# The input projection's token columns in three groups of 264, 512 and 512, and the weights' slots at the tokens' remainder modulo 512 bytes

## The reference

```python
for l in range(DEPTH):                       # DEPTH = 2
    h = _rmsnorm(x, norm1_g[l])
    z = h @ w_in[l]                          # (1024 x 1024) @ (1024 x 2824)
    mq, mk, mv, mi, mf, mo, aq, ak, av = split(z)
    qk = silu(causal_dwconv(concat(mq, mk)))
    hm = mlstm_chunkwise(...)                # 4 heads of 128, chunks of 64
    hm = _rmsnorm(hm) * sigmoid(mo)
    ha = swa_sinks(rope(rmsnorm(aq)), rope(rmsnorm(ak)), av)
    x = x + concat(hm, ha) @ w_out[l]
    h2 = _rmsnorm(x, norm2_g[l])
    x = x + square(relu(h2 @ w_ff1[l])) @ w_ff2[l]
```

## Time and profile before

| | |
|---|---|
| median of 3 runs | 2230.84 us (2230.73 to 2233.3) |
| profiled execution, its own time | 2231.89 us |
| its span | 2230.0 us |
| TensorE clock granted | 0.99 of the full clock |
| PE busy | 2140.7 us, 96% of the span |
| PEld, DVE, POOL, ACT busy | 1805.8, 1424.1, 988.0, 857.6 us |

### The profile page before, as it was taken

How to read it: one execution, slowest core, us unless ns; L and a number is a source line. 1 busy time by engine, 2 the same in 40 slices (tenths; PEclk the granted TensorE clock), 3 DMA queues, 4 the chain that set the end, 5 groups by cost and what they waited for, 6 DMA issues and landing times.

```text
span 2230.0 us, 34286 instructions
## 1 busy us (share of the span) xinstructions
PE 2140.7 (96%) x11748; PEld 1805.8 (81%) x11748; DVE 1424.1 (64%) x1674; ACT 857.6 (38%) x1459; POOL 988.0 (44%) x697
## 2 busy tenths in 40 slices
PE   6999998989999999999999999899899999999998
PEld 6998877878788877888899887788878887778886
DVE  4127865467777777676640488654677777876764
ACT  4224333345666642121231343432556666321210
POOL 3334524324555555445522455143245555454542
PEclk9999999999999999999999999899999999999999
DMA  7322225415777788776532223254166677987663
GB/s 261 105 92 76 72 94 179 136 70 168 255 254 241 239 304 314 306 281 256 215 129 86 90 77 111 83 174 151 39 209 237 237 237 249 348 313 292 270 273 142
DMA packets 227662, 427.29 MB, mean 192 GB/s; under 512 B 24936, under 2 KB 167016, under 8 KB 219248
## 3 DMA queue, kind: packets, MB, share of 16 engines
q1 hardware_dynamic: 212336, 402.93, 51.0%
q10 hardware_dynamic: 15232, 23.16, 2.9%
HBM read 272.79 MB, written 157.43 MB: 193 GB/s over the span
## 4 chain that ended last, share of the span: by engine, by line
PE 58%; issue 19%; POOL 12%; DVE 5%; ACT 2%; SPq 1%; DMA 1%; ACTq 1%; POOLq 0%; DVEq 0%
PE ps L1368 23%; PE ps L1714 20%; POOL w1s L1309 8%; PE ps L1553 7%; POOL w2s L1313 3%; PE ps L1666 1%; DMA uk<-uD 1%; PE ps L1472 1%; DVE y L1756 1%; DVE hT L1762 1%; PE ps L1499 1%; PE ps L1486 1%; PE ps L1591 1%; PE ps L1592 1%; PE ps L1359 1%
## 5 line engine op out<-in xcount | busy, mean ns | idle before, releaser
L1714 PE MATMUL ps<-w2s,uk 128*128 128x512 f32 x2688 | 618.6, 392 | 7.6 <-DVE uf L2249 4.1
L1714 PEld LDWEIGHTS ps<-w2s,uk 128*128 128x128 f32 x2688 | 504.8, 189 | 120.2 <-issue 11.4
L2213 DVE TENSOR_TENSOR xs<-ps,xs 128x1024 f32<-128x1024 f32 x208 | 253.4, 1222 | 171.6 <-PE ps L1714 169.9
L1666 PE MATMUL ps<-hT,w1s 128*128 128x512 f32 x1344 | 317.8, 392 | 10.6 <-DVE uf L2175 4.7
L1666 PEld LDWEIGHTS ps<-hT,w1s 128*128 128x128 f32 x1344 | 250.1, 188 | 73.4 <-issue 12.5
L1313 POOL TENSOR_TENSOR w2s<-raw,w2s 128x1024 fp32r<-128x1024 f32 x64 | 182.0, 2866 | 181.3 <-ACT w2s L1088 181.3
L1309 POOL TENSOR_TENSOR w1s<-rawf,w1s 128x512 fp32r<-128x512 f32 x112 | 170.2, 1531 | 194.3 <-ACT w1s L982 194.3
L1368 PE MATMUL ps<-hT,whi 128*128 128x512 f32 x768 | 246.3, 402 | 0.0
L1368 PE MATMUL ps<-whi,hT 128*128 128x258 f32 x1280 | 238.2, 286 | 1.0 <-DVE hT L1762 0.6
L1666 PE MATMUL ps<-tT,w1s 128*128 128x512 f32 x1008 | 237.3, 389 | 0.0
L1666 PEld LDWEIGHTS ps<-tT,w1s 128*128 128x128 f32 x1008 | 189.1, 188 | 39.5
(11 more groups left out here) (209 smaller groups left out, 3318.7 us busy)
## 6 DMA issues: line engine op xcount, KB each, us to landing
uk<-uD SPq DMA_DIRECT2D x64, 1024.0 KB, 8.7
raw<-in_wstream SPq DMA_DIRECT2D x104, 512.0 KB, 5.6
uk<-uD SPq DMA_DIRECT2D x64, 768.0 KB, 7.8
rawf<-in_wstream SPq DMA_DIRECT2D x64, 512.0 KB, 4.3
uD<-uh SPq DMA_DIRECT2D x64, 512.0 KB, 5.1
uD<-uf SPq DMA_DIRECT2D x64, 512.0 KB, 5.3
uD<-uh SPq DMA_DIRECT2D x64, 384.0 KB, 4.1
uD<-uf SPq DMA_DIRECT2D x64, 384.0 KB, 5.0
```

The costliest lines, as they stand in the source:

```text
L1666: mm = pe.matmul(ps[:, bank, :], w, x[:, k, :], start=(first and k == 0 and i == 0), stop=(k == 3 and i == 2), skip_group_check=True)
L1714: mm = pe.matmul(ps[:, bank + tp, :], u, w2s[r][:, w, k, :], start=(r in (1, 2, 5) and k == 0 and i == 0), stop=(k == 1 and i == 2), skip_ ...
L2213: V.tensor_tensor(y, ps[:, bank:bank + 2, :], y, ALU.add).then_inc(y_acc, 1)
```

## The change

The 1288 columns of stage A are in three groups, GC = 264, 512 and 512: 3 x 8 x 24 = 576 matmuls a layer. Group 0 takes the first 258 columns of z's store and its last six (from column ZX = 1282 on). The host's layout of the weights stays in pieces of 258 columns, so each unit is put together by two or three DMAs. Group 0 still has two units (of four k), groups 1 and 2 have four each (of two k). The high and low parts have places of their own: `ahi0`, `alo0` and `ahi1` where the slots were, `alo1` behind the small tables, `ahi2`, `alo2` in the place of x (`xs`), for which ACT waits until x is normed and stored. The slots of the later stages are 4096 bytes long, and all of them, `ahi1`, `alo1`, `ahi2`, `alo2`, `mxh` and `mxl`, now lie at 224 modulo 512. `ahi0` is at 224 and `alo0` at 480, with slices 1056 bytes apart. Other small tiles move by 128 bytes (`qS`, `kown`, `kw0`, `Cst` and so on). `zst` holds 512 columns.

```diff
+GC = (264, 512, 512)
+ZX = ZV + 512 - 6
...
-        raw = [ring_r(f"raw{s}", [P, 4 * GW], F32) for s in range(RING)]
+        raw = [ring_r(f"raw{s}", [P, 4 * GC[0]], F32) for s in range(RING)]
         hilo_at = ring_r.at
-        whi = [ring_r(f"whi{s}", [P, 4 * GW], F32R) for s in range(RING)]
-        wlo = [ring_r(f"wlo{s}", [P, 4 * GW], F32R) for s in range(RING)]
+        ahi0, alo0 = [ring_r(f"a{n}0", [P, KT, GC[0]], F32R) for n in ("hi", "lo")]
+        ahi1_at = ring_r.at
+        ahi1 = ring_r("ahi1", [P, KT, 512], F32R)
+        br = Region(hilo_at)
+        whi = [br(f"whi{s}", [P, D], F32R) for s in range(RING)]
+        br = Region(ahi1_at)
+        wlo = [br(f"wlo{s}", [P, D], F32R) for s in range(RING)]
+        xr_ = Region(wide.at)
+        ahi2, alo2 = [xr_(f"a{n}2", [P, KT, 512], F32R) for n in ("hi", "lo")]
...
+        alo1 = Region(ahi1_at + (ta.at - ahi1_at + 511) // 512 * 512)("alo1", [P, KT, 512], F32R)
...
-                sp.dma_start(raw[slot][:], wtoken[l, n]).then_inc(s_raw[slot], 16)
+                def piece(g, kh, k0, ks, c0, dst):
+                    src = wtoken[l, 2 * g + kh].rearrange("p (k c) -> p k c", c=GW)
+                    sp.dma_start(dst, src[:, k0:k0 + ks, c0:c0 + dst.shape[2]]).then_inc(s_raw[slot], 16)
+                if n < 2:
+                    d = raw[slot][:].rearrange("p (k c) -> p k c", c=GC[0])
+                    piece(0, n, 0, 4, 0, d[:, :, 0:GW])
+                    piece(4, n, 0, 4, ZX - 4 * GW, d[:, :, GW:GC[0]])
...
-                    nc.scalar.copy(zst[b][:], ps[:, G + t % 2, 0:GW]).then_inc(a_ev, 1)
+                    nc.scalar.copy(zst[b][:, 0:GC[g]], ps[:, G + t % 2, 0:GC[g]]).then_inc(a_ev, 1)
...
-                    if t in (2, 3):
-                        split_a(l, t, 0, 0)
+                    if 2 <= t < 6:
+                        if t == 2 and l > 0:
+                            act.wait_ge(y_m, l * YM)
+                        split_a(l, t)
...
-                group(1, 2)
-                rows_b()
-                group(2, 0)
+                for n in range(NT):
+                    tile(1, n)
+                    if n == 3:
+                        rows_b()
                 rows_t()
-                group(3, 2)
-                rows_m()
-                group(4, 0)
+                for n in range(NT):
+                    tile(2, n)
+                    if n == 3:
+                        rows_m()
```

More of the change, by code:

```diff
@@ L104, in trunk_kernel @@
         ta = Region(tmp_at)
-        zst = [ta(f"zst{b}", [P, GW], F32) for b in range(4)]
+        zst = [ta(f"zst{b}", [P, 512], F32) for b in range(4)]
         gN = ta("gN", [P, NT, 8], F32)
@@ L172, in trunk_kernel @@
         ends = Region((nc.sbuf_usable_end - 3 * 4 * D) // 32 * 32)
[L173 removed]
+        assert max(ta.at + 512 + 4 * KT * 512, tc.at) <= ends.at, (ta.at, tc.at, ends.at)
         ybuf = [ends(f"y{b}", [P, D], F32) for b in range(2)]
@@ L370, in unit_a @@
                 sp.wait_ge(w_lo, l * U + max(n + 1, RING))
-                sp.dma_start(raw[slot][:], wtoken[l, n]).then_inc(s_raw[slot], 16)
+                def piece(g, kh, k0, ks, c0, dst):
[5 more added lines that the diff above has]
+                    piece(4, n, 0, 4, ZX - 4 * GW, d[:, :, GW:GC[0]])
+                else:
+                    kh, k0 = (n - 2) % 4 // 2, (n - 2) % 2 * 2
+                    d = raw[slot][:, 0:D].rearrange("p (k c) -> p k c", c=512)
+                    if n < 6:
+                        piece(1, kh, k0, 2, 0, d[:, :, 0:GW])
+                        piece(2, kh, k0, 2, 0, d[:, :, GW:512])
+                    else:
+                        piece(2, kh, k0, 2, 512 - GW, d[:, :, 0:4])
+                        piece(3, kh, k0, 2, 0, d[:, :, 4:4 + GW])
+                        piece(4, kh, k0, 2, 0, d[:, :, 4 + GW:512])
             def unit(l, n, slot):
@@ L710, in landed, with unit_raw, unit_part, unit_hi @@
             eng.wait_ge(s_raw[slot], (l * (16 * per_layer[slot]) + use * 16) + 16 * (before + 1))
+        def unit_raw(n):
+            return raw[n % RING][:, 0:(4 * GC[0] if n < 2 else D)]
+        def unit_part(n, a0, a1, a2):
+            t, k = (a0, 4) if n < 2 else (a1 if n < 6 else a2, 2)
+            i = n if n < 2 else (n - 2) % 4
+            return t[:, i * k:(i + 1) * k, :].rearrange("p k c -> p (k c)")
+        def unit_hi(n):
+            return unit_part(n, ahi0, ahi1, ahi2)
+        def unit_lo(n):
+            return unit_part(n, alo0, alo1, alo2)
         @block.scalar
         def _(act):
-            def split_a(l, slot, before, use):
-                landed(act, l, slot, before, use)
-                nc.scalar.copy(whi[slot][:], raw[slot][:]).then_inc(w_hi, 1)
+            def split_a(l, n):
+                landed(act, l, n % RING, 2 * (n // RING) + (1 if n < 6 else 2), 0)
+                nc.scalar.copy(unit_hi(n), unit_raw(n)).then_inc(w_hi, 1)
             def split_hi(l, slot, before, use, dst):
@@ L1373, in _, with tile @@
             for l in range(DEPTH):
-                def tile(g, s0, n):
-                    pe.wait_ge(a_ev, l * (5 * NT) + g * NT + (n + 1))
+                def tile(g, n):
+                    pe.wait_ge(a_ev, l * (3 * NT) + g * NT + (n + 1))
                     t = tile_of(l * 2, n) if g == 0 else n
-                    pairs = []
+                    wh, wl = ((ahi0, alo0), (ahi1, alo1), (ahi2, alo2))[g]
                     for k in range(KT):
[L1381 to L1389, removed]
+                        if n == 0:
+                            if g == 0 and k == 0:
+                                pe.wait_ge(w_lo, l * U + (2 + RING))
+                            elif g > 0 and k % 2 == 0:
+                                pe.wait_ge(w_lo, l * U + (4 * g - 2 + k // 2 + 1 + RING))
+                        c = (t % 4) * P
+                        h_, l_ = hT[:, t // 4, 0, k, c:c + P], hT[:, t // 4, 1, k, c:c + P]
+                        for i, (a, b) in enumerate(((h_, wh), (h_, wl), (l_, wh))):
+                            mm = pe.matmul(ps[:, G + n % 2, 0:GC[g]], a, b[:, k, :], start=(k == 0 and i == 0), stop=(k == KT - 1 and i == 2))
+                    mm.then_inc(a_done, 1)
                 if l == 0:
```

73 lines of the change are left out of this document (40 added, 33 removed).

## The result

The changed kernel takes **2238.62 us** (median of 7 runs, 2236.36 to 2239.88) where the kernel before, run beside it, takes 2230.84 (7 runs, 2228.76 to 2234.17). The ratio is 1.0032 with an interval of [1.0022, 1.0042]: 7 us slower. 2224.2 was forecast. The profiled execution took 2238.57 us with a span of 2236.8, against 2231.89 and 2230.0.

What follows compares the result with a forecast made beforehand. PE, busy 96% of the span, was taken as the bound: matmul count by start distance. Gains 20.9 less losses 14.3 net 6.6 us off 2231.9; the median, 1.05 lower, gives 2224.2 us, range 2209 to 2235.

Steps and rivals of the forecast that it cites:

- Head, 14.0: Start of layer 0: small load pieces wait turns behind large packets, PE starts at 36.0 not 21.91; 14.0 us lost.
- Rival 1: Head: not late, as q1's packets are batched or 24-byte runs merged; 2210.8 us, chance 0.13.
- Stage A, 10.6: Stage A: fewer, wider matmuls at 226.7 ns save 5.3 us a layer, 10.6 us in all.
- ACT late in group 0, 0.25 a layer: Stage A, group 0: ACT's 4.2 us at tiles 2 to 4 exceed PE's 3.8; 0.5 us lost in all.
- Rival 3: Stage A: uncosted stalls, ACT late in group 0 or units 6 to 9 late; 4 us more, 2228, chance 0.16.
- POOL's low parts "have eight tiles of time": Stage A, groups 1 and 2: POOL's four low parts a group, 2.9 us each, are hidden; no loss.
- Stage B, 6.0: Stage B: 1152 matmuls each 6.2 ns shorter through operand placement, 7.1 us, of which 6.0 arrive.
- Stage C, 4.3: Stage C: 768 matmuls each 6.2 ns shorter through operand placement, 4.8 us, of which 4.3 arrive.
- Rival 2: B, C and wide groups: place in SBUF doesn't set the distance, which stays 232.9 ns; 2239 us, chance 0.13.
- The MLP, 0: MLP, to the next stage A or the end: no change in time, 0 us.

Runs made afterwards that it cites:

- the best version: Changed kernel with each stage A unit one load, group 0's evacuation one store, and splits of units 4 and 5 at tiles 6 and 7; 2216.01 us.
- e3: Changed kernel with the load of `gB` issued ahead of unit 0's two loads; ratio 1.0017 to the kernel before.
- e1: Changed kernel with each stage A unit laid out by the host as one run per partition, so one load; 2225.61 us.

## Why the prediction was wrong

It had the sign wrong, by 13.4 us of span: 2.1 of them in the head, 6.4 in stage A, 2.9 in B, 0.2 in C and 1.8 in the MLP. By its own steps:

- **Head, 14.0 (with bounds to 16).** The mechanism is right and shown twice (whole units, late copies). Unit 1's split began at 31.69 (about 32 forecast), and with `gB` first PE started at 36.27 (36.0). What was missing is 1.8 us: the prediction named `gB` and DVE's `y` as late "and catch up before unit 1's low part". They didn't, since each `y` stood still beside one of POOL's low parts (6.63 us for two of 1.27).
- **Rival 1** (packets batched) is out: 160 packets against 160.
- **Stage A, 10.6.** This size was right, where nothing else was in the way: the best version saves 5.4 and 5.5 a layer, for 5.3 in the sum. The distance of 226.7 ns was right too.
- **ACT late in group 0, 0.25 a layer.** This is the step that failed. The changed kernel's stage A lacks 127.91 - 126.16 = 1.75 in layer 0 and 131.55 - 126.35 = 5.2 in layer 1 to the best version's: 6.95 us for a term of 0.5, and all of it in group 0. The sum compared ACT's work in a tile (4.2 us, with 0.34 a store) with PE's 3.8, and let PE's lead over the evacuations cover it. The second issue took 0.45 to 1.35 us, and it stands between an evacuation and `norm_hi`, on the way by which PE gets its next tile; PE's lead doesn't help there. In layer 1 later low parts are worth 4.5 us with two stores and nothing (0.1) with one; one store is worth 6.3 with early low parts, 1.9 with late ones. So they cost most together: the second store puts DVE's `y` of tile 7 into the time of POOL's low part, `y` stands for 2 us, PE's gap grows to 2.5, and its clock falls for 3.4 us. The clock's part is about 1.5 us: e3, with a gap of 2.46 but no such stretch behind it, has 34.33 us in group 0 where the changed kernel has 35.84. Rival 3 was this mechanism, priced at 4 us with a chance of 0.16.
- **POOL's low parts "have eight tiles of time".** True for POOL, but DVE waits for it. The prediction asked only if POOL was late. Beside a whole low part `y` took 3.28 us (in e1), beside halves 2.22 and alone 1.27, while `hT`'s low part took its 1.23 beside one (at 1151.40). The Trainium skill's page SBUF — State Buffer (section SBUF: two separate sides) has the rule: GpSimd and a VectorE operation with two inputs in SBUF use one pair of ports, and whoever starts first keeps it for the whole instruction. The trace agrees: `y` (from `xs` and `gB`) and `gN` (from `zst` and `rowp`) are such operations, the low part `hT` (one input from PSUM) is not.
- **Stage B, 6.0.** 3.1 came in the changed kernel. The distance is right (5.48 a unit, 0.11 less; 0.15 forecast): the first matmuls of the unit at 173.91, behind the attention's small ones, start 230, 231, 236, 228, 233 and 231 ns apart, and only then come 226 and 227. 48 units by 0.11 are 5.3, of which 3.1 arrived. In layer 0 one more half-clock stretch fell into the dense part of the stage, at 304 us; the other kernels with these slots took 188.0 to 189.9 there, and over both layers these kernels gained 2.8 to 4.8.
- **Stage C, 4.3**: 4.1, which is in part luck. The ten other kernels with these slots gained 1.5 to 4.0 there. Rival 2 is out for B, C and the wide groups.
- **The MLP, 0.** It is the same program and took 1.7 us longer in layer 1. The windows show where: before, and then after, 19 us behind the first matmul of the stage.

```profile
1598.00:1604.00 6.00, 5.41 (x46) 5.41 (x47) 3.27 (x5) 1.45 (x3) 1.28 (x1) 1.00 0.00 0
```

```profile
1603.00:1609.00 6.00, 5.57 (x34) 5.57 (x35) 2.80 (x4) 0.02 (x1) 1.28 (x1) 0.72 0.00 0
```

34 matmuls in place of 46, at a mean clock of 0.72: half clock for some 3.4 us. In the profiled executions the MLP of layer 1 took 651.1 to 651.3 us in the three kernels whose slots are not at 224 and 652.2 to 654.2 in the eleven whose slots are. Why the clock falls there stays open; no run here was made to steer it.

## What to carry to other kernels

Count a store or a load that is split in two where it is issued: if the issuing engine has to do something behind it that the bound engine waits for, the issue can cost there, whatever slack the engine has in all. Eight second stores of 0.45 us and more cost 0.9 to 1.9 us a layer here, and up to 6.3 with what they pushed into POOL's way. Small pieces in one queue waited a turn each for a large packet of the other (160 to 160, and 14 us in all), so lay the data out for one run on the host, or keep the large copies out of the way. When work of POOL is moved, look at which DVE instructions it now stands beside, and who waits for those.

## What the hardware showed that I had not expected

- The issue of a store of 6 columns took 0.45 us where that of 258 took 0.34, and once 1.35 (at 47.54, in the head). The 6 columns were always the second of two stores, so the runs don't tell whether it is the size or the place.
- DVE's `y` with two inputs in SBUF stands still for the one POOL instruction that runs, and then takes its 1.27 us; halving POOL's instruction halved the wait.
- With operands at one remainder modulo 512, the unit of B at 173.91 comes to a distance of 226 or 227 ns only after seven matmuls; the piece of C at 383.23 does so after three (233 and 231 ns first).
- In five kernels PE stood for 2.45 to 3.40 us (start to start) at tile 7 of layer 1's group 0. Four of them had 3.4 us at 1.2 GHz right behind it; e3, with 2.46, had not.
